# Routing inside the output projection's loop: logits by tile, six tiles chosen there, slot products in four column groups

## The reference, cut to what matters

```python
h_lat = h_lat + g1 * (y @ w_out)
h = modulate(rmsnorm(h_lat, norm_ffn), sh2, sc2)
g_logits = h @ w_rg + b_rg                      # 4 groups
g_sel = argmax(g_logits); g_w = softmax(g_logits)[g_sel]
e_logits = (h @ w_re + b_re)[group g_sel]       # 8 experts of that group
top_v, top_i = top_k(e_logits, 2)
e_w = softmax(top_v) * g_w
# every expert: silu(x @ w_gate) * (x @ w_up) @ w_down on its own tokens, summed by weight
```

## Time and profile before

| | us |
|---|---|
| median of three runs (4203.53, 4207.16, 4208.13) | 4207.16 |
| profiled execution, whole | 4214.54 |
| its span, first to last instruction | 4212.8 |
| PE / DVE / ACT / POOL busy in the span | 3916.2 / 1758.3 / 1380.3 / 707.3 |
| mean granted clock | 0.969 |
| projection loop, first projection to the last (from 3580.3 to 3695.5) | 115.2 |
| from there to the first gather of the experts (3751.17) | 55.7 |

### The profile page before, as it was taken

One profiled execution on the slowest core, in us unless ns is written; L12 is line 12 of the kernel. 1 busy time (PEld: TensorE's weight loads), 2 busy tenths in 40 slices (PEclk: granted clock), 3 DMA queues, 4 the chain that ended last, 5 costly groups with the idle time before them and its releaser, 6 DMA issues.

```text
span 4212.8 us, 44627 instructions
## 1 busy us (share of the span) xinstructions
PE 3916.2 (93%) x16066; PEld 2134.7 (51%) x16066; DVE 1758.3 (42%) x3692; ACT 1380.3 (33%) x3360; POOL 707.3 (17%) x902
## 2 busy tenths in 40 slices
PE   5999899999999999988999997999999999958995
PEld 2444466655444566555465665445556544423332
DVE  2443566345353565354266545012223202343445
ACT  3433555123233554233344444112223312111113
POOL 1012000032012000131043334002212101002331
PEclk8999999999999999999999998999999999979998
DMA  5010210122111231122001002001100110159886
GB/s 239 0 40 21 80 51 21 33 81 71 58 41 41 107 119 37 37 65 102 21 6 37 20 21 90 14 26 52 42 32 21 62 40 30 63 218 386 317 311 229
DMA packets 88167, 346.24 MB, mean 82 GB/s; under 512 B 20984, under 2 KB 52864, under 8 KB 69136
## 3 DMA queue, kind: packets, MB, share of 16 engines
q1 hardware_dynamic: 69520, 304.55, 19.5%
q0 software_dynamic: 18432, 38.85, 2.6%
HBM read 400.91 MB, written 37.83 MB: 104 GB/s over the span
## 4 chain that ended last, share of the span: by engine, by line
PE 75%; DVE 5%; ACT 3%; issue 2%; DMA 2%; POOL 1%; POOLq 0%; DVEq 0%; SPq 0%; ACTq 0%
PE psum L88 33%; PE psum L94 8%; PE psum L1562 6%; PE psum L1983 5%; PE psum L3168 5%; PE psum L881 4%; PE psum L904 4%; PE psum L3190 3%; PE psum L2210 2%; DMA arena<-hn_scratch,arena 1%; PE psum L1399 1%; PE psum L2167 1%; PE psum L312 1%; PE psum L1914 1%; DVE arena L175 0%
## 5 line engine op out<-in xcount | busy, mean ns | idle before, releaser
L88 PE MATMUL psum<-arena 128*128 128x512 f32 (+4 forms) x4704 | 1813.5, 544 | 32.3 <-DVE arena L2715 13.6
L88 PEld LDWEIGHTS psum<-arena 128*128 128x128 f32 (+1 forms) x4704 | 877.3, 188 | 903.2 <-issue 821.3
L94 PE MATMUL psum<-arena 128*128 128x128 f32 (+2 forms) x3024 | 444.4, 281 | 63.3 <-DMA arena<-hn_scratch,arena 8.1
L94 PEld LDWEIGHTS psum<-arena 128*128 128x128 f32 (+2 forms) x3024 | 344.1, 143 | 264.7 <-issue 163.7
L1983 PE MATMUL psum<-arena 128*128 128x512 f32 (+1 forms) x640 | 291.7, 583 | 9.0 <-DVE arena L2011 4.8
L1562 PE MATMUL psum<-arena 128*128 128x512 f32 x576 | 263.9, 607 | 8.4 <-DVE arena L1748 8.4
L3168 PE MATMUL psum<-arena 128*64 x512 | 232.1, 607 | 22.8 <-issue 11.0
L3169 PE MATMUL psum<-arena 128*64 128x512 f32 x512 | 232.2, 607 | 0.0
L175 DVE SCALAR_TENSOR_TENSOR arena<-psum,arena 128x512 f32<-128x512 f32 (+1 forms) x100 | 60.5, 605 | 404.4 <-ACT arena L172 404.4
L170 ACT ACTIVATE arena<-psum 128x512 f32<-128x512 f32 (+1 forms) x100 | 52.9, 529 | 489.8 <-PE psum L88 489.8
L904 PE MATMUL psum<-arena 64*128 64x512 f32 (+1 forms) x800 | 166.2, 547 | 19.1 <-ACT arena L994 11.3
(11 more groups left out here) (395 smaller groups left out, 4797.8 us busy)
## 6 DMA issues: line engine op xcount, KB each, us to landing
arena<-w_gu SPq DMA_DIRECT2D x32, 2048.0 KB
arena<-w_ada SPq DMA_DIRECT2D x24, 2048.0 KB
arena<-w_dn SPq DMA_DIRECT2D x32, 1024.0 KB
arena<-w_in SPq DMA_DIRECT2D x12, 2048.0 KB
arena<-w_out SPq DMA_DIRECT2D x6, 2048.0 KB
arena<-gate_rows_scratch SPq DMA_DIRECT2D x36, 256.0 KB, 3.4
x_scratch<-arena SPq DMA_DIRECT2D x18, 512.0 KB, 3.1
arena<-x SPq DMA_DIRECT2D x16, 512.0 KB, 10.0
```

Source lines behind the costliest of these rows:

```text
L88: ins = e.matmul(out, l, r, start=(i == 0), stop=(i == n - 1))
L94: ins = e.transpose(o, i, idn)
```

## The change

1. Tables of the router are loaded by SP ahead of the residual rows of tile 2 instead of behind those of tile 7.
2. PE's loop: the turn of tile t-1 stands between the two halves of tile t. Behind the second half stand the logits of tile t-1: eight matmuls of 128 columns, alternating between two column groups (partitions 0 and 64) that each hold half of the sum. ACT copies both parts; a matmul with a doubled identity (`foldl`) adds them and turns them (`pe_logits_turn`), two tiles behind. DVE adds the bias per tile. PSUM banks of the turned rows are two instead of four.
3. DVE chooses tiles 0 to 5 in the loop's pass for tile 7, and tiles 6 and 7 in the routing stage.
4. The expert number comes from the first index kept by the choice instead of from a product and a sum.
5. Slot products: BL is stationary (32 wide), SL moves (128 columns), in four column groups, in two halves as SL comes; ACT copies, and a matmul with a four-fold identity (`foldb`) adds and turns.
6. SP waits for the logits of tile 7. Buffers are placed anew.

```diff
--- before.py
+++ after.py
@@ -2795,11 +2795,12 @@
             load_w(e, ("out2", 1), I["w_out2"][1], 512, proj.of("merge_b", "br", 1, 7))
             all_met(e, ("merged", "br"))
             for t in range(NL_T):
+                if t == 2:
+                    e.wait_ge(*acop.of("gate_row2", 7))
+                    sp_route(e)
                 if t >= 2:
                     e.wait_ge(*vmul.of("out2x", t - 2, 1))
                 e.dma_start(xr2[:, t % 2, :], X2[tile(t), :]).then_inc(*rows_in[t % 2].by("res2", t))
-            e.wait_ge(*acop.of("gate_row2", 7))
-            sp_route(e)
             for t in range(NL_T):
                 e.wait_ge(*vmul.of("hn", t))
                 e.dma_start(HN[tile(t), :], Yc[:, t, :]).then_inc(*hn_out[t].by(t))
@@ -2825,14 +2826,44 @@
                             e.wait_ge(*w_ready(("out2", g)))
                         mm(e, P[2 * (t % 2) + g], [(OT[:, k, tile(t)], w[g][:, k, :]) for k in range(8)]
                            ).then_inc(*proj.by("out2", t, g))
-                if t:
-                    u = t - 1
-                    e.wait_ge(*vmul.of("hn", u))
-                    for h in range(2):
-                        if u >= 2:
-                            e.wait_ge(*(vcop if h else acop).of("hn", u - 2))
-                        turn(e, [(P[4 + 2 * (u % 2) + h][:, tile(j)], Yc[:, u, tile(4 * h + j)]) for j in range(4)], ident
-                             ).then_inc(*turned.by("hn", u, h))
+                        if g == 0 and t:
+                            if t >= 2:
+                                pe_logits_turn(e, t - 2)
+                            pe_hn_turn(e, t - 1)
+                    if t:
+                        pe_logits(e, t - 1)
+                else:
+                    pe_logits_turn(e, t - 2)
+                    pe_hn_turn(e, t - 1)
+                    pe_logits(e, t - 1)
+                    pe_logits_turn(e, t - 1)
+
+        def pe_hn_turn(e, u):
+            e.wait_ge(*vmul.of("hn", u))
+            for h in range(2):
+                if u:
+                    e.wait_ge(*(vcop if h else acop).of("hn", u - 1))
+                turn(e, [(P[4 + h][:, tile(j)], Yc[:, u, tile(4 * h + j)]) for j in range(4)], ident
+                     ).then_inc(*turned.by("hn", u, h))
+
+        def pe_logits(e, u):
+            if u == 0:
+                e.wait_ge(*stage_in.of("route"))
+            else:
+                e.wait_ge(*acop.of("logits", u - 1))
+            e.wait_ge(*acop.of("hn", u))
+            e.wait_ge(*vcop.of("hn", u))
+            for k in range(8):
+                r = 64 * (k % 2)
+                ins = e.matmul(P[6][r:r + 36, 0:128], wr[:, k, :], OT[:, k, tile(u)], start=(k < 2), stop=(k >= 6))
+            ins.then_inc(*proj.by("logits", u))
+
+        def pe_logits_turn(e, u):
+            e.wait_ge(*vsta.of("foldl"))
+            e.wait_ge(*acop.of("logits", u))
+            if u:
+                e.wait_ge(*vmul.of("logits", u - 1))
+            e.matmul(P[7][:, 36 * u:36 * u + 36], lgT, foldl, start=True, stop=True).then_inc(*turned.by("logits", u))
 
         def a_out2(e):
             a_row(e, ("gate_row2",), gtr2, 8, P[0:4])
...
-                        ins = e.activation(OT[:, j, tile(u)], P[4 + 2 * (u % 2)][:, tile(j)], ACT.Identity,
+                        ins = e.activation(OT[:, j, tile(u)], P[4][:, tile(j)], ACT.Identity,
                                            bias=MOD2[:, 24 + j, 0:1], scale=AF[:, j:j + 1])
                     ins.then_inc(*acop.by("hn", u))
+                    a_logits(e, u)
                 if t < NL_T:
                     s_ = ss2[:, t:t + 1]
                     e.wait_ge(*vmul.of("out2x", t, 1))
...
+        def a_logits(e, u):
+            e.wait_ge(*proj.of("logits", u))
+            if u:
+                e.wait_ge(*turned.of("logits", u - 1))
+            else:
+                e.wait_ge(*gmul.of("lgT"))
+            for r in (0, 64):
+                ins = e.activation(lgT[r:r + 36, :], P[6][r:r + 36, 0:128], ACT.Copy)
+            ins.then_inc(*acop.by("logits", u))
+
         def v_out2(e):
             v_row(e, ("gate_row2",), MOD2[:, 16:24, 0], 8)
+            e.tensor_tensor(foldl, ident[:, 0:36], ident[:, 64:100], ALU.add).then_inc(*vsta.by("foldl"))
             for t in range(NL_T):
...
-                        ins = e.tensor_scalar(OT[:, 4 + j, tile(u)], P[5 + 2 * (u % 2)][:, tile(j)],
+                        ins = e.tensor_scalar(OT[:, 4 + j, tile(u)], P[5][:, tile(j)],
                                               AF[:, 4 + j:5 + j], MOD2[:, 28 + j, 0:1], ALU.mult, ALU.add)
                     ins.then_inc(*vcop.by("hn", u))
                 if t < NL_T:
                     s_ = ss2[:, t:t + 1]
...
                     e.tensor_scalar(Yc[:, t, :], XO[:, t, :], s_, None, ALU.mult).then_inc(*vmul.by("hn", t))
+                if 2 <= t < NL_T:
+                    v_logits(e, t - 2)
+                if t == NL_T - 1:
+                    v_choose(e, 0, 6)
+
+        def v_logits(e, u):
+            e.wait_ge(*stage_in.of("route"))
+            e.wait_ge(*turned.of("logits", u))
+            e.tensor_tensor(LG[:, u, :], P[7][:, 36 * u:36 * u + 36], br, ALU.add).then_inc(*vmul.by("logits", u))
+
+        def v_choose(e, a, b):
+            n = b - a
+
+            def step(ins):
+                vo.seq(e, ins)
+
+            def pick_first(oh, val, vmax, m, r_, t_):
+                step(e.tensor_tensor(oh, val, bc(vmax, m), ALU.is_equal))
+                step(e.tensor_tensor(oh, oh, mid(r_, n), ALU.mult))
+                step(e.tensor_reduce(t_, oh, AX, ALU.max))
+                step(e.tensor_tensor(oh, oh, bc(t_, m), ALU.is_equal))
...
+            e.wait_ge(*vmul.of("logits", b - 1))
+            step(e.tensor_reduce(s_[:, 0], gl, AX, ALU.max))
+            pick_first(g_, gl, s_[:, 0], 4, rev[:, 0:4], s_[:, 1])
+            e.tensor_tensor(x_, gl, bc(s_[:, 0], 4), ALU.subtract).then_inc(*vsta.by("gx", a))
...
+            step(e.tensor_reduce(s_[:, 4], m1, AX, ALU.max))
+            pick_first(oh1, m1, s_[:, 4], 32, rev[:, 4:36], s_[:, 5])
+            step(e.scalar_tensor_tensor(m2, oh1, -3e30, m1, ALU.mult, ALU.add))
+            step(e.tensor_reduce(s_[:, 6], m2, AX, ALU.max))
+            pick_first(oh2, m2, s_[:, 6], 32, rev[:, 4:36], s_[:, 7])
+            step(e.tensor_tensor(MS[:, ts], oh1, oh2, ALU.add))
+            if a == 0:
+                step(e.memset(PS[:, 0, :], 0.0))
+            for t in range(a, b):
+                ins = e.tensor_tensor(PS[:, t + 1, :], PS[:, t, :], MS[:, t, :], ALU.add)
+                if t < b - 1:
+                    step(ins)
+            ins.then_inc(*vsta.by("chosen", a))
+            e.wait_ge(*vsta.of("chosen", a))
...
@@ -2923,18 +3017,9 @@
             e.dma_start(wr, I["w_router"]).then_inc(*stage_in.by("route"))
 
         def pe_route(e):
-            e.wait_ge(*stage_in.of("route"))
-            e.wait_ge(*acop.of("hn", NL_T - 1))
+            b = P[4]
+            e.wait_ge(*vsta.of("chosen", 6))
             e.wait_ge(*vcop.of("hn", NL_T - 1))
-            for k in range(8):
-                for g in range(2):
-                    ins = e.matmul(P[0][64 * g:64 * g + 36, :], wr[:, k, :], OT[:, k, half(g)], start=(k == 0), stop=(k == 7))
-            ins.then_inc(*proj.by("logits"))
-            e.wait_ge(*acop.of("logits"))
-            e.wait_ge(*vcop.of("logits"))
-            turn(e, [(P[1][:, tile(j)], lgT[:, tile(j)]) for j in range(4)], ident).then_inc(*turned.by("logits"))
-            b = P[4]
-            e.wait_ge(*vsta.of("chosen"))
...
-            e.wait_ge(*vmul.of("slots"))
-            for n in range(16):
-                ins = e.matmul(P[5][:, 0:NB], SL[:, n, :], BL[:, n, :], start=(n == 0), stop=(n == 15))
+            for hf in range(2):
+                e.wait_ge(*vmul.of("slots", hf))
+                for n in range(8 * hf, 8 * hf + 8):
+                    j = n % 4
+                    ins = e.matmul(P[5][32 * j:32 * j + 32, 0:128], BL[:, n, :], SL[:, n, :], start=(n < 4), stop=(n >= 12))
             ins.then_inc(*prod.by("slots"))
+            e.wait_ge(*acop.of("slots"))
+            e.matmul(P[3][:, 0:NB], slT, foldb, start=True, stop=True).then_inc(*prod.by("slotsT"))
 
         def a_route(e):
-            e.wait_ge(*proj.of("logits"))
-            e.wait_ge(*gmul.of("lgT"))
-            e.activation(lgT[0:36, :], P[0][0:36, :], ACT.Copy).then_inc(*acop.by("logits"))
-            e.wait_ge(*vsta.of("gx"))
+            e.wait_ge(*vsta.of("gx", 0))
+            e.wait_ge(*vsta.of("gx", 6))
...
+            e.wait_ge(*prod.of("slots"))
+            e.activation(slT, P[5][:, 0:128], ACT.Copy).then_inc(*acop.by("slots"))
 
...
-            oh1, oh2 = OH[:, 0], OH[:, 1]
-            e.wait_ge(*stage_in.of("route"))
-            e.wait_ge(*gmul.of("lgT"))
-            e.wait_ge(*proj.of("logits"))
-            e.tensor_copy(lgT[64:100, :], P[0][64:100, :]).then_inc(*vcop.by("logits"))
```

(74 more changed lines are left out.)

7 lines of the change are left out of this document (added).

## The result

The changed kernel takes 4244.9 us (median of four runs, 4239.0 to 4251.7) against 4207.7 us for the kernel before (four runs): 1.0084 times as long, 95% interval 1.0066 to 1.0102, some 37 us. Forecast were 4239 us with 4224 to 4248 as the range. Its profiled execution took 4251.7 us, with a span of 4249.6 (before: 4212.8).

The account below looks back on a forecast made before the run. PE, never idle, bounds the projection loop, then a chain mostly on VectorE up to the first gather, with which the expert stage moves. Loop +36.6, then +3.0, -5.7, -2.0 give +31.9 on the median 4207.2: 4239 us, range 4224 to 4248.

Parts of the forecast that it names:

- waits of PE, six: Projection loop: PE waits 3.1 us per tile for VectorE's copies of the turned rows, six tiles, 18.7 us.
- clock, six falls: Projection loop: PE's clock falls to 1.2 GHz after waits, 1.7 us each, five falls of six, 8.5 us.
- logits, fold, changes, one turn: Projection loop, PE's added work: logits 5.4, folding turn 1.3, wide-narrow changes 1.8, one row turn 0.9 us.
- to the scaled rows: Last projection to scaled rows: 7.5 us instead of 4.5, as the square follows the delayed logits' copy; +3.0.
- to the choice: Scaled rows to end of choice: 18.6 us instead of 24.3, the early choice's gain mostly put back; -5.7.
- to the gather: Choice to first gather: index steps save 1.1, slots 1.1, halved slot table costs 0.2; -2.0 us.
- expert stage: After the first gather: the stage moves as a whole with that gather and keeps its length.
- the wait is not there: Rival, loop: copies finish before PE's second half ends, no stall or clock fall; +1 us, 4208; chance 0.09.
- the clock holds: Rival, loop: PE waits but keeps full clock, without the 8.5 us; +23, 4230; chance 0.18.
- Dearer than that: Rival: all six clock falls, loop logits without overlap, last logits 3.5 us; +40, 4247; chance 0.10.
- the cap of 1.1 us: Slot products before the gather: gain 0.2 to 1.15 us, taken 1.1, since VectorE's other steps cover the rest.
- the tables do not matter: Rival, expert stage: first blocks wait for weights, not gathers, absorbing a late gather; +17, 4224; chance 0.06.

Follow-up runs that it names:

- e3: Changed kernel with seven unused matmuls of 224 columns filling PE's wait before each tile's logits in the loop; 1.0045 times the kernel before.
- e1: Changed kernel with VectorE's copies of the turned tile t-1 moved between the output steps of tile t's two halves; 1.0002 times the kernel before.
- e4: Changed kernel with the choice of tiles 0 to 5 moved behind the copies of tile 7; one run, scaled rows to choice 19.2 us for 18.8.
- e2: e1 with five tiles chosen in tile 6's pass, three behind the loop, and logits copied behind the square on ScalarE; 0.9991 times the kernel before.
- e6: Kernel before with only the kept expert index and the four-group slot products in halves (parts 4 and 5); 0.9999 times the kernel before.
- e5: e2 with the last gate row's tables and the choices' weights moved into VectorE's idle time; 0.9993 times the kernel before.
- e7: The changed kernel run again without edits; 1.0084 times the kernel before, expert stage 466.4 us.

## Why the prediction was right, step by step

| term (us) | predicted | measured | where |
|---|---|---|---|
| waits of PE, six | 18.7 | 18.1 | loop of e3 less e1; 2.94 each in the changed kernel |
| clock, six falls | 8.5 | 9.3 | loop of changed less e3 |
| logits, fold, changes, one turn | 9.4 | 9.1 | loop of e1 less before |
| to the scaled rows | +3.0 | +3.6 | table |
| to the choice | -5.7 | -5.5 | table |
| to the gather | -2.0 | -2.3 | table |
| sum | +31.9 | +32.4 | table; the first gather moved from 3751.17 to 3783.63 |
| expert stage | 0 | +4.4 | table; it moved with the gather, but did not keep its length |

**The wait.** It was read from the fixed order of VectorE's program and one row of before, L2883 ending 3.0 us after PE was free. e1 shows that this order is the cause. The rival "the wait is not there" put the kernel at 4208, +1 us; e1 makes exactly that case: its sum is 1.1 us above before.

**The clock.** I took five falls of six; it fell every time, and 1.55 us were lost each time rather than 1.7. The gap of 2.85 us that had kept full clock was the exception it looked like. The rival "the clock holds" falls for this kernel.

**To the scaled rows.** 0.6 us more than forecast, because the logits in front of the square took 1.93 us, all at the lower clock, where I had put 1.3.

**Logits.** 0.9 was taken at full clock, 1.01 measured (e1). At the lower level 1.93 were predicted as 1.9 for the last tile. "Dearer than that" asked for 1.74 at full clock, which is out. The changes between wide and narrow were priced at 0.3 a tile; 0.23 is what was left for them. The Trainium skill, "TensorEngine Tiling (Array Packing)", section Key Properties, says that a change of tiling mode drains TensorE. e1's trace neither shows nor excludes a drain; it leaves room for about 0.1 us a change.

**The choice.** The number held (18.8 for 18.6), one reason did not. That the steps' fixed part is paid twice is right: the choice takes 8.3 and 5.5 us where one took 9.65. That the large piece was harmful because it stood before a wait of PE is wrong by e4: behind the wait it cost as much. It sat on the end because all of VectorE's steps do; e2 takes them off by choosing in the pass before.

**The slots.** PE's product became 4.8 us shorter (2.22 for 7.03, including the wait for the second half of the table) but choice to gather only 2.3 (e6). What PE's gain could give was VectorE's wait of 1.16 us for it in the earlier trace rows, and that wait is gone: the cap of 1.1 us held. The Trainium skill, "TensorEngine Tiling (Array Packing)", section Performance Considerations, advises to swap the operands and use four-fold column tiling; the estimate from it was 1.8 us for the product, and the trace has 2.22.

**The expert stage** does move with the gather, and "the tables do not matter" falls: in e1, e2 and e5, whose gathers come 31 to 39 us earlier than the changed kernel's after the loop's beginning, its length stays within 3 us. But "keeps its length" was too strong: my reasons, landed weights and an empty DMA, bear on the stage's start and not on its length. The length varies from 458.6 to 466.4 between the profiles, and in the changed kernel it is 4.4 us above before (4.8 in e7), which my sum did not have. Most of what the forecast of 4239 is low by comes from there. That it still fell into the range owes something to the width of the range, which was made for other terms.

## What to carry to other kernels

Where an engine is busy all the time, ask of every instruction put into its queue what it waits for, and look up where that producer stands in the *other* engine's program, not only how long it takes: here four copies in the wrong place of VectorE's order cost 27 us in the loop, waits and clock together, and 4 us behind it; moving them took all of it back. A wait of 3 us on TensorE is priced together with the half-rate stretch that the trace shows behind it, here a further half of the wait (1.55 us for 2.94); filling it with useless matmuls is a quick test of that share. Work is taken off a serial end only if it goes where its engine idles; one place earlier in the same chain, or a shorter product beside longer steps of another engine, changes little.

## What the runs showed of the hardware that was not expected

- The granted clock fell behind every one of the seven waits of 2.94 us, in a loop in which PE was otherwise never idle; with the wait filled down to 0.30 us (e3) it stayed at 1.00 in the loop.
- 36-wide logits of 128 columns in two column groups took 1.01 us for eight matmuls at full clock (e1). A quarter of the 512-column pace gives 0.86, no overlap at all 1.74, so here the two groups keep most of their overlap at 128 columns, not all.
- The expert stage's length lay between 458.6 and 466.4 us in eleven profiles, and most of the difference arose before the eighth block's rows were stored. Two profiles of the same code (changed, e7) agreed within 0.5 us; two kernels with the first gather 1.3 us earlier or later gave 463.1 and 458.6, one profile each.
